# First expert matmul in three sweeps, and light units' gate half drained one piece later

## What is computed

```python
def swiglu(x, wg, wu, wd):
    return (jax.nn.silu(x @ wg) * (x @ wu)) @ wd      # x: (256, 1024), wg, wu: (1024, 3584), wd: (3584, 1024)

def moe_swiglu(x, w_router, we_gate, we_up, we_down):
    logits = (x @ w_router).astype(jnp.float32)
    top_vals, top_idx = lax.top_k(logits, TOP_K)
    gates = jax.nn.softmax(top_vals, axis=-1)
    combine = jnp.einsum("bske,bsk->bse", jax.nn.one_hot(top_idx, N_EXPERTS, dtype=jnp.float32), gates)
    ...
    for e in range(N_EXPERTS):
        out = out + combine[..., e:e + 1] * swiglu(x, we_gate[e], we_up[e], we_down[e])
```

## Time and profile before

| | |
|---|---|
| time of three runs | median 1282.41 us (1281.19 to 1285.21) |
| time of the profiled execution | 1281.19 us, the lowest of the three |
| its span, first to last instruction | 1279.5 us, so 1.7 us lie around it |
| mean granted TensorE clock | 0.997 of full speed |
| expert stage | about 374 us to 1262 us of the span |
| bytes moved | 434.49 MB, mean 340 GB/s |

### The profile page before, as it was taken

How to read it: one execution, slowest core, us unless ns; L and a number is a source line. 1 busy time by engine, 2 the same in 40 slices (tenths; PEclk the granted TensorE clock), 3 DMA queues, 4 the chain that set the end, 5 groups by cost and what they waited for, 6 DMA issues and landing times.

```text
span 1279.5 us, 15891 instructions
## 1 busy us (share of the span) xinstructions
PE 1222.3 (96%) x6199; PEld 1051.8 (82%) x6199; DVE 1112.1 (87%) x871; ACT 937.3 (73%) x720; POOL 50.0 (4%) x57
## 2 busy tenths in 40 slices
PE   9999999999999999999999999999999999999785
PEld 8988888888989888888787877878888788887563
DVE  6978555568889999999999999999999999999897
ACT  5575444454867787888878888888888778878774
POOL 0100000001010000000000000000000000000130
PEclk9999999999999999999999999999999999999998
DMA  9947655537459999999999999999999999999992
GB/s 320 343 161 263 195 183 184 195 122 244 169 173 342 376 409 394 403 412 410 410 405 406 411 410 413 407 394 409 412 410 410 410 404 411 409 412 402 411 412 116
DMA packets 143556, 434.49 MB, mean 340 GB/s; under 512 B 8964, under 2 KB 50996, under 8 KB 131188
## 3 DMA queue, kind: packets, MB, share of 16 engines
q1 hardware_dynamic: 139936, 421.07, 85.7%
q0 software_dynamic: 3456, 12.32, 2.8%
q10 hardware_dynamic: 84, 0.02, 0.0%
HBM read 428.40 MB, written 4.98 MB: 339 GB/s over the span
## 4 chain that ended last, share of the span: by engine, by line
PE 59%; DMA 17%; DVE 16%; ACT 5%; issue 3%; SPq 0%; DVEq 0%; ACTq 0%
DVE w_lo L1027 13%; DMA raw<-in_we_down 9%; PE turn L1691 7%; PE turn L1693 6%; PE turn L1692 6%; DMA raw<-in_we_gate 6%; PE accp L1691 5%; PE accp L1692 5%; PE accp L1693 5%; PE turn L1803 4%; PE turn L1800 4%; ACT w_hi L657 4%; PE turn L1802 2%; PE turn L1801 2%; PE turn L2117 2%
## 5 line engine op out<-in xcount | busy, mean ns | idle before, releaser
L1027 DVE TENSOR_TENSOR w_lo<-raw,w_hi 128x1792 fp32r<-128x1792 f32 (+3 forms) x449 | 900.8, 2040 | 93.1 <-ACT w_hi L657 87.7
L657 ACT CAST w_hi<-raw 128x1792 fp32r<-128x1792 f32 (+2 forms) x443 | 760.0, 1725 | 171.0 <-DMA raw<-in_we_down 42.5
L2117 PE MATMUL turn<-w_hi,t_both 128*128 128x448 f32 x512 | 192.9, 377 | 25.3 <-DVE w_lo L1027 18.0
L2118 PE MATMUL turn<-w_lo,t_both 128*128 128x448 f32 x512 | 186.9, 365 | 0.0
L1691 PE MATMUL turn<-w_hi,a_hi 128*128 128x448 f32 x496 | 183.9, 371 | 0.0
L1693 PE MATMUL turn<-w_hi,a_lo 128*128 128x448 f32 x496 | 181.7, 366 | 0.0
L1692 PE MATMUL turn<-w_lo,a_hi 128*128 128x448 f32 x496 | 181.6, 366 | 0.0
L2117 PEld LDWEIGHTS turn<-w_hi,t_both 128*128 128x128 f32 x512 | 96.1, 188 | 49.1 <-issue 19.6
L2118 PEld LDWEIGHTS turn<-w_lo,t_both 128*128 128x128 f32 x512 | 96.3, 188 | 7.2
L1691 PEld LDWEIGHTS turn<-w_hi,a_hi 128*128 128x128 f32 x496 | 93.1, 188 | 9.6
L1692 PEld LDWEIGHTS turn<-w_lo,a_hi 128*128 128x128 f32 x496 | 93.2, 188 | 8.4
(11 more groups left out here) (291 smaller groups left out, 1539.5 us busy)
## 6 DMA issues: line engine op xcount, KB each, us to landing
raw<-in_we_gate SPq DMA_DIRECT2D x128, 896.0 KB, 8.6
raw<-in_we_up SPq DMA_DIRECT2D x128, 896.0 KB, 9.3
raw<-in_we_down SPq DMA_DIRECT2D x96, 1024.0 KB, 9.5
raw<-in_w_in SPq DMA_DIRECT2D x18, 1024.0 KB, 7.0
raw<-in_we_down SPq DMA_DIRECT2D x32, 512.0 KB, 6.2
raw<-in_w_down SPq DMA_DIRECT2D x11, 1024.0 KB, 5.0
raw<-in_w_gate SPq DMA_DIRECT2D x10, 1024.0 KB, 5.2
raw<-in_w_up SPq DMA_DIRECT2D x10, 1024.0 KB, 5.3
```

The lines of the kernel that those rows point to most:

```text
L657: nc.scalar.copy(w_hi[:, p % PARTS, 0:filled(p)], raw[:, p % RING, 0:filled(p)]).then_inc(hi_done, 1)
L1027: return nc.vector.tensor_tensor(out, whole, hi.bitcast(f32), ALU.subtract)
L2117: nc.tensor.matmul(to[:, c, :], few, wh[:, kk, c, :], start=(k == 0), stop=False)
L2118: last = nc.tensor.matmul(to[:, c, :], few, wl[:, kk, c, :], start=False, stop=(k == KD - 1))
```

## The change

It has three edits, all in the expert stage.

1. In `first_gate`, after the 16 hi by hi matmuls, all 16 hi by lo come next (four for each piece, waiting for that piece's split), and then all 16 lo by hi; `piece_used` is added to in the last sweep, after each piece's four.
2. On ACT, in light units, hi of b + 2 (and `keep_ys` where there is one) comes ahead of `leave_gate`, and `silu_few` comes one piece earlier: after hi of b + 3, not of b + 4. For heavy units the new lines give the same order as the old.
3. On PE, in light units, `add_low(i, 0)` comes after the first up piece, ahead of the first down piece (in the last unit, after the first up piece instead of the second).

```diff
@@ ACT, loop over the units
-                splits(b, b + 1)
-                if light(i):
-                    leave_gate(i)
-                split_hi(b + 2)
+                splits(b, b + 2)
                 if kept_at(i) is not None:
                     keep_ys(kept_at(i))
-                if not light(i):
-                    leave_gate(i)
+                leave_gate(i)
                 if i in (1, 2):
                     scale_tokens(i - 1)
...
-                silu_at = b + 4 if light(i) else b + 3
-                splits(b + 3, silu_at)
+                split_hi(b + 3)
                 if light(i):
                     silu_few(i)
-                splits(silu_at + 1, min(unit_end, ahead))
+                splits(b + 4, min(unit_end, ahead))
...
-            splits(b + 3, b + 4)
+            split_hi(b + 3)
             silu_few(N_UNITS - 1)
-            splits(b + 5, down_piece(N_UNITS - 2, 1))
+            splits(b + 4, down_piece(N_UNITS - 2, 1))
@@ PE, first_gate, after the hi by hi sweep
-                for pair in range(4):
-                    pe.wait_ge(*split_of(MOE_AT + pair))
-                    pe.wait_ge(xg_lo_ready, pair // 2 + 1)
-                    for k in (2 * pair, 2 * pair + 1):
-                        for c in range(2):
-                            nc.tensor.matmul(gate_banks[:, c, :], xg_hi[0][:, k, :], w[pair][1][:, k % 2, c, :],
-                                             start=False, stop=False)
-                            last = nc.tensor.matmul(gate_banks[:, c, :], xg_lo[0][:, k, :], w[pair][0][:, k % 2, c, :],
-                                                    start=False, stop=(k == KD - 1))
-                    last.then_inc(piece_used, 1)
+                for k in range(KD):
+                    if k % 2 == 0:
+                        pe.wait_ge(*split_of(MOE_AT + k // 2))
+                    for c in range(2):
+                        nc.tensor.matmul(gate_banks[:, c, :], xg_hi[0][:, k, :], w[k // 2][1][:, k % 2, c, :],
+                                         start=False, stop=False)
+                for k in range(KD):
+                    if k % 4 == 0:
+                        pe.wait_ge(xg_lo_ready, k // 4 + 1)
+                    for c in range(2):
+                        last = nc.tensor.matmul(gate_banks[:, c, :], xg_lo[0][:, k, :], w[k // 2][0][:, k % 2, c, :],
+                                                start=False, stop=(k == KD - 1))
+                    if k % 2:
+                        last.then_inc(piece_used, 1)
@@ PE, loop over the units
-                    if light(i) and place == 1:
+                    if light(i) and place == 0:
                         add_low(i, 0)
```

## The result

| | kernel before | changed kernel |
|---|---|---|
| time, median of 4 runs each on one chip | 1282.36 us (1281.19 to 1285.21) | 1292.44 us (1290.77 to 1293.57) |
| ratio (95% interval) | | 1.0075 (1.0053 to 1.0096) |
| time and span of the profiled execution | 1281.19 and 1279.5 us | 1285.44 and 1283.7 us |
| mean granted TensorE clock in it | 0.997 | 0.993 |

The changed kernel is slower by 0.75%, about 9.6 us by the ratio (the two medians lie 10.1 us apart). The forecast was 1283.8 us and no change that can be measured; the time lies above the range of 1278 to 1288.

The account below looks back on a forecast made before the run. DMA at a fixed 408 GB/s was taken to bound the long stretch, TensorE the time before 440 us. The profiled 1281.19 + 1.7 - 0.3 = 1282.6 us; as a median, 1282.41 + 1.4 = 1283.8 us, range 1278 to 1288.

Parts of the forecast that it names:

- The stall: First gate: TensorE waits 1.7 us for the first up piece, and everything up to 440 us moves by that.
- The silu waits: Light units, a sign of being right: rows of waits for the silu line shrink to below 4 us.
- TensorE gains up to a microsecond in each of 16 light units: Light units: net of the earlier silu, some 1.5 us sooner, and the `add_low` push of about 0.6 us.
- the push of `add_low`: Light units: few_low is written later, so `add_low` pushes TensorE's next matmuls by about 0.6 us.
- a sign that I would be wrong: Light units: a wait of TensorE for few_low of more than 1 us a unit would show the forecast wrong.
- ACT's waits for the DMA: Long stretch: 42.5 us over 63 down pieces before; forecast to grow as TensorE's gain turns into waiting there.
- The gain of 0.3 us from the weak stretch: DMA after the first light unit: 0.3 us gained of 0.63 us lost there, with 0 and 0.6 as ends.
- The rival in which TensorE's waits are the bound: Long stretch paced by TensorE's silu waits: removing them gives 7.2 to 18.4 us, time 1265.7 to 1276.9; chance 0.08.
- the 7.2 and the 11.2 us: Light units: TensorE's silu waits (9 times) and its weight loads' waits (11 times), added to 18.4 us in a rival.
- The rival in which the moved drain starves the queue: Light units: `leave_gate` behind the cast holds TensorE up to 1.69 us each; 1296 to 1309 us; chance 0.07.
- The gather does not depend on the silu. Cost and gain 0: Last unit: silu about 2.3 us sooner, but VectorE waits for the last gathered rows, so the end does not move.
- My tail rival: Kernel end: the last gather lands 4 to 6 us sooner or later, 1278 or 1289; chance 0.09, half each side.

Follow-up runs that it names:

- drain_early: light_only with the drain of the gate bank back ahead of the third cast, silu and `add_low` still early; 1282.19 us, ratio 0.9992 to the kernel before.
- sweeps_only: The kernel before with only the three sweeps of edit 1; 1284.5 us, ratio 1.0005 to the kernel before.
- add_low_late: light_only with `add_low(i, 0)` back behind the first down piece, so edit 2 without edit 3; 1303.9 us, ratio 1.0151 to the kernel before.
- light_only: The changed kernel with the old `first_gate`, so edits 2 and 3 alone; 1289.61 us, ratio 1.0051 to the kernel before.
- last_unit_new: The kernel before with the new order (drain, silu, `add_low`) in the last unit only; 1290.53 us, ratio 1.0051 to the kernel before.
- last_drain_only: The kernel before with only the drain moved behind the third cast, in the last unit only; 1292.23 us, ratio 1.0057 to the kernel before.
- pause_for_gather: The changed kernel with VectorE waiting for ACT's drain before the split of b + 2 in the last unit; 1283.13 us, ratio 1.0000 to the kernel before.
- the first group: The first four experiments (sweeps_only, light_only, drain_early, add_low_late) and the kernel before run next to them, which took 1283.79 us.

## Why the prediction was wrong, point by point

**Edit 1: right.** ACT's cast, VectorE's split and TensorE's first matmul of the up piece came at 382.52, 384.32 and 386.40 us, where 382.31, 384.11 and 386.2 were forecast, all later by the 0.2 us by which the stage began later. The stall was forecast at 1.7 us; the matmul starts 1.86 us later than before (1.49 us of waiting in the row), 1.66 without these 0.2, and in time the edit costs 0.6 us (-0.5 to +1.9).

**Edits 2 and 3 in the long stretch: right in the bound, wrong in what TensorE gains.** The silu waits fell below 4 us, 408 GB/s stayed, and drain_early, which takes nearly all of these waits away, wins nothing beyond its interval: the DMA hides them. "TensorE gains up to a microsecond in each of 16 light units" is false: the push of `add_low` was put at 0.6 us, and 12 waits for `few_low` of about 1 us each came in place of silu waits that were smaller in sum, 12.2 against 7.2 us. I had named such a wait as a sign that I would be wrong; it lies under the full queue as well. ACT's waits for the DMA fell where I said that they would grow. The gain of 0.3 us from the weak stretch at 496 to 504 us is too small for the times to show; the rate there was 404 and 398 GB/s in the changed profile, against 383 and 372, but sweeps_only, which lacks edits 2 and 3, has 406 in the first of the two windows as well.

The rival in which TensorE's waits are the bound is false. Its price was too high as well: TensorE's matmuls and its weight loads wait for the same silu at the same time (in the last unit both go on at 1242.07 us), so the 7.2 and the 11.2 us do not add up. The rival in which the moved drain starves the queue is false for this change, by the rate; add_low_late shows what it looks like when it happens, at 399 GB/s and a ratio of 1.0151. It named the instruction that costs, the drain, but with another mechanism and in all 16 units in place of one.

**The tail: the step that failed.** "The gather does not depend on the silu. Cost and gain 0". The silu is indeed not what it depends on. How long it takes depends on a pause of VectorE, and edit 2 took the only one away: with the drain behind the third cast, the cast is in time, VectorE splits piece b + 2 without its 0.1 us of idling, and GpSimd's instruction is held to VectorE's next stop. That stop is VectorE's own wait for these rows. The row was in my hands as 8.81 us in the earlier trace rows, against 3.58 us of idling before it; I took it for an issue that costs what it costs, and didn't ask what its end followed. The term stood at 0; it measured +6.5 us in light_only (0.0051 of 1283.79 us), +6.6 in last_unit_new and +7.3 in last_drain_only. My tail rival had the right place, and nearly the size (4 to 6 us, 1289), but no mechanism, and with it half of 0.09.

Behind these rows may stand a rule that I should have weighed: the Trainium skill ("SBUF — State Buffer", SBUF: two separate sides) says that VectorE and GpSimd share a pair of SBUF ports under an exclusive lock, and that a VectorE operation with two SBUF inputs contends for it with a GpSimd operation that reads SBUF. The splits have two SBUF inputs, `raw` and `w_hi`, and the gather takes its row numbers from SBUF. The traces agree in direction: 0.94 us with VectorE idle, 8.81 and 16.09 us with it busy. They differ in two things. The same page, in Who interferes with whom, says that `tensor_tensor`, which is what the splits are, did not stall a DMA; here the gather's instruction stood for 8 to 16 us behind splits. And the page has the loser go on some 115 ns after VectorE's instruction ends; here the last gather was not let through at the ends of splits whose successor starts 0.07 us ahead of them, and it finished 0.8 us after the first hand-over without that overlap. The lock as the cause is thus not shown; what the runs show is that the pause decides.

**Why the profiled execution of the changed kernel was faster than its timed ones.** In it the load of piece b + 2 landed at 1237.79 us, so ACT waited 0.55 us for it, and VectorE was held a little after all: its three splits take 5.96 us, above the dense 5.88, and the gather ends at 1240.35, 8.81 us after its start. Whether the last unit has its pause may then be a matter of the DMA's timing in each execution. That the timed runs at 1290.77 to 1293.57 us had lost the pause fits light_only and last_unit_new, but no trace of such an execution of the changed kernel itself was taken.

**What stays open.** Of the 9.6 us, about 6.5 to 7 go to the gather, and 0.6 to edit 1; the rest, some 2 us, is within the intervals and is not assigned. The 6.5 us are themselves not the wait alone: all six executions of light_only have a mean granted clock of 0.991 or less, and those of the kernel before at such a clock have a median of 1285.4 us, so at like clock light_only is 4.2 us slower. The rest goes with the clock, a part of it with the fall behind the wait; how much was not separated. What lets the gather through is not fully known either. In the kernel before, the gathers that start at 1188.79 and 1223.11 us end 0.84 and 0.81 us after the end of a split as well (2.97 and 2.47 us in all), but there the next VectorE instruction had started 0.08 us ahead, as in a row without a pause. Moving the gather to another engine's queue was not tried.

## What to carry to other kernels

Before you take a wait away from a busy engine, look for whoever lives off its pauses: a GpSimd instruction whose duration is many times that of its kind (here 8.81 us, where the three before it took 0.99 to 2.97) may be waiting, although it counts as busy. Ask of it what ends it, and read that from where it ends, not from where it starts. In the tail nothing hides such a change, and one instruction moved by one place can be worth more than 16 units' waits under a full DMA queue.

## What the runs showed of the hardware

- The same gather instruction on GpSimd took 0.94, 8.81 or 16.09 us, by where VectorE paused. A split that started some 0.05 us later than it does in a dense row was enough for the 8.81 (pause_for_gather); a pause of 0.1 us did the same in the kernel before.
- When TensorE stood waiting for 7.31 to 9.59 us, as the late gather makes it, the granted clock fell to 0.50 and was there for 9 us and more (light_only, last_unit_new, last_drain_only); the steps between the next matmuls were 0.42 us in place of 0.23.
- The granted TensorE clock also fell to its lower level, 1.2 of 2.4 GHz, while TensorE was multiplying without a gap. In the changed kernel's profile it does so from 1201.9 to about 1205 us, where the matmuls had gone on since 1200.01 us, after a wait of 1.51; there a matmul takes 0.58 us in place of 0.36, and the steps between starts are 0.37 in place of 0.20:

```profile
1201.45 0.36 PE L2112 MATMUL turn<-w_hi,t_both 128*128 128x448 f32 x1
...
1202.91 0.58 PE L2113 MATMUL turn<-w_lo,t_both 128*128 128x448 f32 x1
...
1203.28 0.58 PE L2112 MATMUL turn<-w_hi,t_both 128*128 128x448 f32 x1
```

- Twelve of the fourteen profiles have such stretches ahead of their last 15 us; those of the kernel before and of drain_early have none. They go with the time of one and the same kernel: of the 23 runs of the kernel before in the first group, the seven at a mean clock of 0.996 or more took 1281.7 us on average, and the eight at 0.990 to 0.991 took 1285.5. So 3.8 us of the spread go with the clock, as much as the 0.3% that a measurement can tell. The clock does not stand for the whole of the gather's 6.5 us: the profiles of light_only and of pause_for_gather have the same mean clock, 0.990, at 1289.06 and 1284.06 us.
